# First two gathers issued from the routing stage, one-hot tables built four tiles at a time, and experts and combination in one block

## The reference

```python
group_logits = h @ w_group + b_group;  grp = argmax(group_logits)          # 4 groups
exp_logits = (h @ w_router + b_router)[grp];  top_p, top_i = top_k(softmax(exp_logits), 2)
weight = p_group[grp] * top_p / sum(top_p);   eid = grp * 8 + top_i        # 32 experts
...
hid = silu(xb @ w_gate[e]) * (xb @ w_up[e]);  y = hid @ w_down[e]          # 1024 -> 512 -> 1024
y_token += weight * y                                                     # two experts per token
...
out = layer_norm(alpha * z + gate * y) * g + b                            # the last residual
```

## Time and profile before

| | us |
|---|---|
| median of 3 runs (lowest, highest) | 2052.57 (2050.16, 2053.76) |
| the profiled execution | 2056.4 |
| its span, first to last instruction | 2054.6 |
| PE busy (share of the span) | 1846.1 (90%) |
| DVE busy | 1449.7 (71%) |
| ACT busy | 1054.2 (51%) |
| POOL busy | 364.2 (18%) |
| mean granted clock of PE, of full speed | 0.947 |

### The profile page before, as it was taken

The page is one execution under the profiler, slowest core; times in us unless marked ns, Lnnn a source line. Parts: engine busy times, 40 slices in busy tenths (PEclk is TensorE's granted clock), DMA queues, the critical chain, the costliest instruction groups (busy, mean ns, idle before and its releaser), DMA issues. The chain is left out here.

```text
span 2054.6 us, 35259 instructions
## 1 busy us (share of the span) xinstructions
PE 1846.1 (90%) x14112; PEld 1045.2 (51%) x14112; DVE 1449.7 (71%) x1849; ACT 1054.2 (51%) x1271; POOL 364.2 (18%) x237
## 2 busy tenths in 40 slices
PE   4988869989969999899999999359999999999955
PEld 1655554434439999873444455324444444444422
DVE  5545555675877666536575778869999988888928
ACT  1455552255433323324333411058888888888824
POOL 0000000011101112110000000024444444444300
PEclk9999999999989999999999999579999999999977
DMA  8500007473263313006132222369999999999925
GB/s 311 99 22 22 1 1 287 154 266 118 102 208 90 90 49 86 11 2 197 51 103 74 91 76 78 123 263 391 401 404 411 414 400 402 392 390 388 359 98 193
DMA packets 164743, 391.33 MB, mean 190 GB/s; under 512 B 25324, under 2 KB 102757, under 8 KB 136960
## 3 DMA queue, kind: packets, MB, share of 16 engines
q1 hardware_dynamic: 148480, 353.68, 47.8%
q0 software_dynamic: 16128, 35.76, 4.6%
HBM read 361.68 MB, written 48.68 MB: 200 GB/s over the span
## 5 line engine op out<-in xcount | busy, mean ns | idle before, releaser
L2162 PE MATMUL ps<-w_gate_up_split,gathered_t 128*128 128x512 f16 x1728 | 388.3, 382 | 4.9 <-ACT gathered_t L2226 4.4
L2295 DVE SCALAR_TENSOR_TENSOR w_gate_up_split<-w_staged,w_gate_up_split 128x2048 f16<-128x2048 f32 x144 | 328.0, 2287 | 54.6 <-ACT w_gate_up_split L2217 52.9
L2217 ACT ACTIVATE w_gate_up_split<-w_staged 128x2048 f16<-128x2048 f32 x144 | 274.4, 1908 | 68.9 <-PEq L144 30.4
L2162 PEld LDWEIGHTS ps<-w_gate_up_split,gathered_t 128*128 128x128 f16 x1728 | 167.9, 98 | 204.7 <-issue 6.6
L217 PE MATMUL ps<-u_transposed,w_gates_split 128*128 128x512 f16 x1152 | 254.7, 383 | 5.7 <-PEq L144 3.0
L813 PE MATMUL ps<-u_transposed,w_dense_split 128*128 128x512 f16 x1152 | 253.7, 382 | 4.3 <-DVE w_dense_split L188 3.5
L2189 PE MATMUL ps<-w_down_split,hidden_t 128*128 128x512 f16 x864 | 196.6, 385 | 7.1 <-ACT hidden_t L2263 4.2
L217 PEld LDWEIGHTS ps<-u_transposed,w_gates_split 128*128 128x128 f16 x1152 | 113.3, 99 | 146.7 <-issue 14.7
L813 PEld LDWEIGHTS ps<-u_transposed,w_dense_split 128*128 128x128 f16 x1152 | 112.7, 99 | 147.3 <-issue 11.4
L2295 DVE SCALAR_TENSOR_TENSOR w_down_split<-w_staged,w_down_split 128x2048 f16<-128x2048 f32 x72 | 164.2, 2287 | 17.8 <-ACT w_down_split L2217 17.6
L2217 ACT ACTIVATE w_down_split<-w_staged 128x2048 f16<-128x2048 f32 x72 | 137.2, 1908 | 43.8 <-DMA w_staged<-in_w_down 20.6
(11 more groups left out here) (356 smaller groups left out, 2943.2 us busy)
## 6 DMA issues: line engine op xcount, KB each, us to landing
w_staged<-in_w_gate SPq DMA_DIRECT2D x72, 1024.0 KB, 11.3
w_staged<-in_w_up SPq DMA_DIRECT2D x72, 1024.0 KB, 10.7
w_staged<-in_w_down SPq DMA_DIRECT2D x72, 1024.0 KB, 10.6
w_dense_ring<-in_w_in SPq DMA_DIRECT2D x17, 1024.0 KB, 6.9
w_ada_ring<-in_w_ada SPq DMA_DIRECT2D x8, 2048.0 KB
w_gates_ring<-in_w_in SPq DMA_DIRECT2D x24, 512.0 KB, 6.5
qkv_scratch<-qkv_silu POOLq DMA_DIRECT2D x20, 512.0 KB, 3.7
w_ada_early<-in_w_ada SPq DMA_DIRECT2D x4, 2048.0 KB, 20.8
```

Of the source, the lines that this page charges most:

```text
L2162: last = pe.matmul(ps[:, GU[s] + j, :], xt[:, s, xp, k, :], w16[:, j, wp, k, :], start=(k == 0 and t == 0), stop=(k == KC - 1 and t == 2))
L2217: nc.scalar.activation(split(kind, 0, int(q)), staged(m, kind, int(q)), ACT.Identity, scale=W_SCALE).then_inc(hi_ok[kind + q], 1)
L2295: nc.vector.scalar_tensor_tensor(split(kind, 1, int(q)), staged(m, kind, int(q)), W_SCALE, split(kind, 0, int(q)), ALU.mult, ALU.subtract) ...
```

## The change

It has four parts. (1) In route, the one-hot tables are built four tiles at a time: per group one compare for `rhs`, one for `lhs`, and two multiplies, each over all four tiles, with room for all 16 tiles instead of a ring of 4. The `m.blocks` steps move behind the slot tables. (2) POOL, idle in route before, clears `xg` there, waits for the slot tables, copies two columns of tokens at once and issues the gathers of blocks 0 and 1; `gather` in experts starts at block 2, and the DVE memset is gone. (3) For block 0 alone, `copy_x` goes ahead of the up splits on ACT and ahead of the low part of gate's second half on DVE. (4) combine's code moves into the experts block, with its tiles laid over dead ones; SP waits on `all_stored`, which POOL raises, loads the result rows and stores the result tiles too. The arithmetic is the same.

```diff
-        lhs = m.sb("slot_one_hot", [P, 4, P], ctx=ctx)
-        rhs = m.sb("block_one_hot", [P, 4, 2, NB], ctx=ctx)
+        lhs = m.sb("slot_one_hot", [P, 2 * TC, P], ctx=ctx)
+        rhs = m.sb("block_one_hot", [P, 2 * TC, 2, NB], ctx=ctx)
...
             for n in range(2 * TC):
-                pe.wait_ge(pairs, n + 1)
+                pe.wait_ge(pairs, n // 4 + 1)
...
+        @block.gpsimd
+        def _(pool):
+            nc.gpsimd.memset(m.xg[:], 0.0).then_inc(cleared, 1)
+            pool.wait_ge(slots_ok, 1)
+            nc.gpsimd.tensor_copy(m.idx[:], m.slot_token[:, 0:2]).then_inc(idx_ready, 1)
+            pool.wait_ge(idx_ready, 1)
+            pool.wait_ge(cleared, 1)
+            for s in range(2):
+                pool.indirect_dma_start(m.xg[:, s].rearrange("p h d -> p (h d)"), None, m.u2_dram.rearrange("t h d -> t (h d)"),
...
-            for n in range(2 * TC):
-                if n >= 4:
-                    dve.wait_ge(table_mm, n - 3)
-                ts(lhs[:, n % 4, :], iota, slot_f[:, n:n + 1], None, ALU.is_equal)
-                ts(rhs[:, n % 4, 0, :], iota[:, 0:NB], blk_f[:, n:n + 1], m.const("token")[:, n:n + 1], ALU.is_equal, ALU.mult)
-                ts(rhs[:, n % 4, 1, :], iota[:, 0:NB], blk_f[:, n:n + 1], w_f[:, n:n + 1], ALU.is_equal, ALU.mult).then_inc(pairs, 1)
+            for n in range(0, 2 * TC, 4):
+                g = slice(n, n + 4)
+                step(tt(rhs[:, g, 0, :], over(iota[:, 0:NB], 4), b3(blk_f[:, g], NB), ALU.is_equal))
+                step(tt(lhs[:, g, :], over(iota, 4), b3(slot_f[:, g], P), ALU.is_equal))
+                step.settle()
+                then(tt(rhs[:, g, 1, :], rhs[:, g, 0, :], b3(w_f[:, g], NB), ALU.mult))
+                tt(rhs[:, g, 0, :], rhs[:, g, 0, :], b3(m.const("token")[:, g], NB), ALU.mult).then_inc(pairs, 1)
...
+            dve.sem_inc(slots_ok, 1)
+            then(tt(cmpe[:], b3(iota[:, 0:NB - E], E), over(end, NB - E), ALU.is_ge))
...
+            sp.wait_ge(all_stored, 1)
+            for c in range(TC):
+                if c >= RING:
+                    sp.wait_ge(added, c - RING + 1)
+                sp.dma_start(ys[:, c % RING], y_view[:, c]).then_inc(y_in[c % RING], 16)
+            for c in range(TC):
+                sp.wait_ge(res_ok, c + 1)
+                sp.dma_start(out_view[:, c, :], res[:, c % 3, :]).then_inc(out_done[c % 3], 16)
...
             for s in range(2):
                 pool.wait_ge(y_stored[s], (j + 2) * 16)
                 pool.sem_inc(pool_turns, 1)
+
+            pool.sem_inc(all_stored, 1)
...
-                    split_high("up", i, s)
-                    copy_x(i, s)
+                    if exists(i, s, 1):
+                        split_high("up", i, s)
+                        copy_x(i, s)
+                    else:
+                        copy_x(i, s)
+                        split_high("up", i, s)
...
-            nc.vector.memset(xg[:], 0.0).then_inc(S("cleared"), 1)
...
         m.reuse_sems()
-        experts(nc, m, a)
-        late.close()
-        combine(nc, m, a, out)
+        experts(nc, m, a, out)
```

More of the change, by code:

```diff
@@ L2006, in load_piece, with experts @@
     sp.dma_start(staged(m, kind, q).rearrange("p (k n) -> p k n", k=k), weight_piece(a, kind, e, q)).then_inc(m.piece_in[kind + str(q)], 16)
-def experts(nc, m, a):
+def experts(nc, m, a, out):
+    RING = 4
     HALF = KC // 2
@@ L2094, in _ @@
                 load("down", j + 1, s)
+            sp.wait_ge(all_stored, 1)
[6 more added lines that the diff above has]
+                sp.dma_start(out_view[:, c, :], res[:, c % 3, :]).then_inc(out_done[c % 3], 16)
+            for s in range(3):
+                sp.wait_ge(out_done[s], 16 * len(range(s, TC, 3)))
         @block.gpsimd
@@ L2125, in work @@
                     store(*back(i, s, 3))
-            pool.wait_ge(S("cleared"), 1)
             turns(pool, work)
@@ L2205, in _ @@
             down(j + 1, 1)
+            for c in range(TC):
+                pe.wait_ge(y_in[c % RING], 16 * (c // RING + 1))
+                if c >= 4:
+                    pe.wait_ge(sum_used, c - 3)
+                for half in range(2):
+                    for k in range(2):
+                        last = pe.matmul(ps[:, 2 * (c % 4) + half, :], m.ident[:], ys[:, c % RING, k, half * 512:half * 512 + 512],
+                                         start=(k == 0), stop=(k == 1))
+                last.then_inc(added, 1)
         @block.scalar
@@ L2511, in build @@
             m.stage = late.enter_context(nc.sbuf_tensor("w_staged", [P, 6, 2048], F32, side="right"))
+            m.xg = late.enter_context(nc.sbuf_tensor("gathered", [P, 2, 2, D], F16, side="right"))
+            m.idx = late.enter_context(nc.sbuf_tensor("slot_token_now", [P, 2], U32, side="right"))
+            m.x_in = [nc.alloc_semaphore(name=f"moe_x_in{s}") for s in range(2)]
             m.piece_in = {n: nc.alloc_semaphore(name=f"moe_{n}_in") for n in PIECES}
```

155 lines of the change are left out of this document (66 added, 89 removed).

## The result

The changed kernel takes **2037.61 us** (median of 4 runs, 2036.19 to 2041.03), the kernel before 2051.74 us in the runs beside it. The ratio is 0.9927, 95% interval 0.9908 to 0.9945: 14.1 us faster, where 12.3 were forecast. The total was met, but by terms that were off on both sides, and so in part by luck. The profiled execution took 2041.0 us with a span of 2039.2 us.

What follows compares the result with a forecast made beforehand. The experts loop was taken as TensorE-bound, leaving only stretches where TensorE starves: routing to first product, and last scatter to combine. 5.2 + 6.1 + 1.0 = 12.3 us off 2052.57 gave 2040.3 us, range 2033 to 2048.

Steps and rivals of the forecast that it cites:

- a stretch of VectorE ahead of the tables that had grown: Sign of being wrong: in route, VectorE's stretch ahead of 1323.85 us, before the tables, grows.
- a loop in which TensorE is not at 100 of 100 us: Sign of being wrong: in the experts loop, TensorE is no longer busy for 100 of 100 us.
- Gathers in route, the drain: Route's exit: GpSimd's drain ends 8.14 us behind the last gather's issue, at 1344.9; ScalarE starts at 1346.3 instead of 1339.5.
- Rival 1: Route's exit: the drain behind the gathers costs nothing; head gains 9.5 to 12.3 us, total 2035 us; chance 0.24.
- First product behind ScalarE's start: Start of experts: first product 5.15 us after ScalarE's start, at 1351.45 instead of 1356.62, 5.2 us earlier.
- One-hot tables: Route: four groups take 7.08 us instead of 10.08; with the block table behind, slots are ready 4.1 us earlier.
- Block table moved: Route: its 2.35 us run beside GpSimd's longer gathers; without that cover, still no loss.
- Rival 4, the memset: Head of route: GpSimd's memset of `xg` stalls VectorE by 2.1 us, total 2042.4 us; chance 0.05.
- The loop is left as it is: Experts loop from block 2 on: TensorE busy 100.00 of 100 us, code unchanged, nothing to be had there.
- One block for experts and combine: From last scatter to combine: GpSimd's drain leaves the path, SyncE's first load goes out 6.1 us earlier.
- The end: Last store: by SyncE, 2.6 us to landing instead of 2.9, and no GpSimd drain of 0.71 follows; 1.0 us.
- the forecast's mechanism: Whole kernel: route's drain ends 8.14 us behind the last gather's issue, total 2040.3 us; chance 0.46.

Runs made afterwards that it cites:

- wait_landing: Changed kernel with GpSimd waiting for both gathers to land before leaving route; route's drain 0.22 us, slot weights to first product 12.35 us, no ratio.
- late_gathers: Changed kernel with the first two gathers, index copy and clearing (on VectorE) moved back into experts; ratio 0.9942 against the kernel before.
- many_dmas: Changed kernel with GpSimd waiting for both gathers, plus twenty extra small GpSimd DMAs early in route; route's drain 1.85 us, no ratio.
- light_loads: Changed kernel with w_down loads at half their bytes from the second block on, so only its time is of use; ratio 0.9890 against the kernel before.
- two_blocks: Changed kernel with combine in its own block again, with own memory and GpSimd output stores; ratio 0.9973 against the kernel before.
- no_drain: Changed kernel with route's block closed without GpSimd's drain; ratio 0.9914 against the kernel before.

## Why the prediction was right in its total, and where its steps were wrong

Two of its own signs of being wrong came up: a stretch of VectorE ahead of the tables that had grown, and a loop in which TensorE is not at 100 of 100 us. By the marks the profiled executions differ by 753.9 - 736.4 = 17.5 us, less the 2.1 us by which the stages ahead of B ran later: 15.4 us. The forecast said 12.3. Step by step:

- **Gathers in route, the drain**: wrong. "The nearest row is the one behind the indirect scatter, so I take its 8.14 us from the last issue." The drain ended 3.5 us behind it. What the row held was not a property of indirect DMAs but the count of 72 of them; here there were 2. The values needed for the rule were in the trace of before: 72, 50, 8 and no DMAs, 5.95, 4.15, 0.71 and 0.03 us. (A fourth exit, with no DMA and 3.67 us, has another cause; see the last section.) I read kinds where I should have counted. Rival 1 had the cheap drain right, by the wrong reason (that it costs nothing): it costs the flight of both gathers. With some 3.3 us from issue to landing (the first gather of after 3.33, the second of wait_landing 3.25) instead of the 8.7 of the first gather before, S to P fell by 6.3 us where the prediction gave it 1.1.
- **First product behind ScalarE's start**: right. 5.15 us predicted, 4.94 measured. No run puts the old order of the first block back, so what the moved `copy_x` is worth by itself is not shown.
- **One-hot tables**: right, a little small. 9.4 us from the first table instruction to S instead of 10.2 (0.36 and 0.68 us for the two forms, groups 1.66 us apart because of overlap, a wait for TensorE of 1.68). With 14.3 before: 4.9 us instead of 4.1. TensorE needed 6.55 us for its 32 matmuls, so the pace of 0.316 each was VectorE's, as assumed.
- **Block table moved**: right. It ran from 1337.4 to 1339.8, covered by the gathers up to 1343.4; where the cover went (late_gathers) it cost its 2.5 us.
- **Rival 4, the memset**: given 0.05, and it came true, with 1.9 us. The section "SBUF: two separate sides" of the page SBUF — State Buffer in the Trainium skill goes further than I had used it. Against a GpSimd instruction that only writes, it says, VectorE is held in its two-port modes and not by having two SBUF inputs. The trace agrees: beside the memset the six instructions of 0.19 us were reductions or had two inputs, and the one that was held was a tensor_scalar with one. Which mode it ran in the trace does not say.
- **The loop is left as it is**: wrong. "Nothing is to be had there" overlooked that something can be lost there. The windows of before showed the DMA engines at 1.01 of the stretch, and from 1774 us on its own turns were over 16.88 us by 2.8 in sum. Relative to B the head gained 9.3 us at P and 6.25 at T: 3.1 us went into waits for weights. Over the runs 64 to 95% of what an edit moved at P arrived at T (in many_dmas all of it), each by one execution. light_loads shows what the turns wait for.
- **One block for experts and combine**: right. The last scatter's issue to the first sum was to be 6.1 us shorter and is, 13.45 to 7.36; two_blocks gives 5.9 back.
- **The end**: right. 1.0 us predicted, 1.2 measured. But the rivals missed how close it was: the same merge with GpSimd's stores would have paid 7.0 us there.
- **Not in the sum**: T to C is 2.8 us shorter, because the last products ran at the higher clock for longer, and the steps from F to L 1.1 us.

Together: 12.3 + 5.2 (drain and gathers) + 0.8 (tables) - 1.9 (memset) - 3.1 (weights) + 2.8 (clock) + 1.3 (steps of the combine and the end) = 17.4 us, of the 17.5. What the gathers and the tables gave beyond the forecast (6.0) and what the memset and the weights took (5.0) nearly cancel. The 4.1 us left were in no term: the clock of the last products, which no edit here orders, and steps at the end. The marks are 5.2 us from the forecast; the median of the runs, 14.1 us, is only 1.8 from it. That closeness is luck and bears out no term; the chance of 0.46 for the forecast's mechanism was too high.

## What to carry to other kernels

Before pricing the exit of a block, count the DMAs that GpSimd has issued since its last exit: here each cost 0.082 us on top of the wait for those in flight, and skipping the drain of experts passed its bill to the next exit (behind route, where the clearing of semaphores drains as well, two DMAs were not passed on). Put it where other engines work on inside the same block, and give the last stores to another queue. A stage in which TensorE is at 100% can still be one that gives gains back: look at the DMA share beside it, and ask whether the stream that feeds it starts earlier too. Here it started 2.7 us later, since the splits that free its buffers stood behind the barrier.

## What the runs showed of the hardware that I had not expected

- The drain's law held over eight counts, from 2 DMAs (0.221 us) to 80 (6.605 us), plain and indirect alike. One drain ahead of route stands outside it: 3.67 us at the end of an earlier stage in which GpSimd had issued no DMA. By the timeline of before it lasts as long as GpSimd's own last instructions, which end at 891.42, and the drain at 891.49:

```profile
889.53 1.89 POOL L1470 TENSOR_TENSOR state_decayed<-state,exp_g_last 128x1024 f32<-128x1024 f32 x1
```

```profile
L1079 POOLq DRAIN  x1: 3671/3671/3671, 887.8 to 887.8; - x1
```

- Not every drain waits for landings: in no_drain the one in the clearing of semaphores took 0.61 us and was over 0.9 us before the first gather landed.
- A 3.51 us memset on GpSimd held a 128x32 tensor_scalar on VectorE to its own end (2.05 us instead of 0.18), and let neighbours with two inputs and reductions pass at 0.19 us.
- The last two groups of 24 down products, behind pauses of 2.2 to 3.4 us and of 3.5 us of TensorE, took 5.34 and 6.8 us in some kernels and 7.03 and 7.04, or 6.7 and 8.2, in others; light_loads had 5.34 and 8.21. Full clock (2.4 GHz) is 5.34; in after the granted clock of 1961 to 1971 was 0.96 and of before's 1965 to 1975 it was 0.83. Neither the length of the pause ahead (2.33 us before one of 7.03, 3.02 before one of 5.34) nor any edit orders them. T to C ranges from 37.7 to 41.8 us by it, more than most of the edits here are worth. What chooses stays open.
